# Two encoder layers on one core: statistics on TensorE, weight splits, and group D's row permutation by SBUF transfers

## The reference

```
for each of 2 layers:
  h = LN0(alpha*h + 0.5*SwiGLU_0(h))                    # D_MODEL 1024, D_FF 2816
  h = LN1(alpha*h + W_o [A(h) | B(h) | C(h) | D(h)])    # four groups of four heads
  h = LN2(alpha*h + 0.5*SwiGLU_1(h))
layer_norm: (x - mean) * rsqrt(var + eps) * g + b
group D:    cq -> rms_norm -> @ w_uq -> per head 64 plain + 32 rotated dimensions (rope)
            ckv -> rms_norm -> @ w_ukv -> keys and values; softmax over visible chunks
rope:       [x1*cos - x2*sin, x2*cos + x1*sin]          # x1, x2: the two halves of a head
```

## Time and profile before

| | |
|---|---|
| median of 3 runs | 1152.07 us (1151.99 to 1152.39) |
| the profiled execution | 1151.99 us, its span 1150.2 us |
| busy, share of the span | PE 1132.4 us, 98%; PEld 96%; DVE 60%; ACT 47%; POOL 8% |
| chain that ended last | PE 88%, DVE 7%, ACT 3%, issue 2% |
| granted TensorE clock | 9 tenths or more in all 40 slices |

### The profile page before, as it was taken

The page is one execution under the profiler, slowest core; times in us unless marked ns, Lnnn a source line. Parts: engine busy times, 40 slices in busy tenths (PEclk is TensorE's granted clock), DMA queues, the critical chain, the costliest instruction groups (busy, mean ns, idle before and its releaser), DMA issues.

```text
span 1150.2 us, 20743 instructions
## 1 busy us (share of the span) xinstructions
PE 1132.4 (98%) x8616; PEld 1099.7 (96%) x8616; DVE 684.9 (60%) x929; ACT 541.5 (47%) x770; POOL 86.4 (8%) x84
## 2 busy tenths in 40 slices
PE   9999999999999999999999999999999999999998
PEld 8999999978899999999999999999788989999997
DVE  6545445778659754545585544467777596454443
ACT  6343443464755634344373434345547565344332
POOL 1000000100161000000100000010003310000001
PEclk9999999999999999999999999999999999999999
DMA  9554444432433545444445544443433425444431
GB/s 346 184 178 151 173 146 159 165 128 91 152 114 117 211 149 182 148 163 165 148 149 189 175 157 162 165 151 117 166 109 132 150 79 216 158 171 154 159 126 42
DMA packets 28788, 178.20 MB, mean 155 GB/s; under 512 B 3568, under 2 KB 3632, under 8 KB 11056
## 3 DMA queue, kind: packets, MB, share of 16 engines
q1 hardware_dynamic: 26976, 171.36, 43.6%
q0 software_dynamic: 1744, 5.88, 1.5%
HBM read 171.79 MB, written 4.25 MB: 153 GB/s over the span
## 4 chain that ended last, share of the span: by engine, by line
PE 88%; DVE 7%; ACT 3%; issue 2%; DMA 0%; SPq 0%; ACTq 0%; DVEq 0%
PE ps L505 26%; PE ps L507 26%; PE ps L506 26%; ACT w_high L1136 2%; DVE z L1626 1%; DVE w_low L1465 1%; DVE w_low L1478 1%; PE ps L795 1%; PE ps L952 1%; PE ps L953 1%; PE ps L954 1%; DVE z L1616 1%; DVE zx_low L1606 1%; DVE x_low L1641 1%; PE ps L910 1%
## 5 line engine op out<-in xcount | busy, mean ns | idle before, releaser
L505 PE MATMUL ps<-x_high,w_high 128*128 128x288 f32 x1536 | 455.5, 297 | 3.9 <-DVE w_low L1465 3.1
L507 PE MATMUL ps<-x_high,w_low 128*128 128x288 f32 x1536 | 453.1, 295 | 0.0
L506 PE MATMUL ps<-x_low,w_high 128*128 128x288 f32 x1536 | 453.1, 295 | 0.0
L1465 DVE TENSOR_TENSOR w_low<-raw,w_high 128x2048 fp32r<-128x2048 f32 (+3 forms) x150 | 326.6, 2180 | 208.8 <-ACT w_high L1136 208.5
L1136 ACT ACTIVATE w_high<-raw 128x2048 fp32r<-128x2048 f32 (+2 forms) x166 | 302.6, 1827 | 113.8 <-PE ps L507 107.7
L505 PEld LDWEIGHTS ps<-x_high,w_high 128*128 128x128 f32 x1536 | 288.4, 188 | 8.3 <-issue 3.9
L507 PEld LDWEIGHTS ps<-x_high,w_low 128*128 128x128 f32 x1536 | 288.5, 188 | 0.0
L506 PEld LDWEIGHTS ps<-x_low,w_high 128*128 128x128 f32 x1536 | 288.3, 188 | 0.1
L505 PE MATMUL ps<-hid_high,w_high 128*128 128x288 f32 x704 | 208.4, 296 | 0.0
L506 PE MATMUL ps<-hid_low,w_high 128*128 128x288 f32 x704 | 208.0, 295 | 0.0
L507 PE MATMUL ps<-hid_high,w_low 128*128 128x288 f32 x704 | 207.9, 295 | 0.0
(11 more groups left out here) (318 smaller groups left out, 1143.2 us busy)
## 6 DMA issues: line engine op xcount, KB each, us to landing
raw<-weights SPq DMA_DIRECT2D x138, 1024.0 KB, 4.9
raw<-weights SPq DMA_DIRECT2D x16, 768.0 KB, 4.3
raw<-weights SPq DMA_DIRECT2D x4, 968.0 KB, 4.7
raw<-weights SPq DMA_DIRECT2D x6, 512.0 KB, 4.1
raw<-weights SPq DMA_DIRECT2D x8, 256.0 KB, 6.2
out_k<-kT POOLq DMA_DIRECT2D x2, 864.0 KB, 4.5
raw<-weights SPq DMA_DIRECT2D x2, 640.0 KB, 5.5
hT<-x_in SPq DMA_DIRECT2D x4, 288.0 KB, 5.5
```

The costliest lines, as they stand in the source:

```text
L505: pe.matmul(out, wh, xh, start=first, stop=False, skip_group_check=True)
L506: pe.matmul(out, wh, xl, start=False, stop=False, skip_group_check=True)
L507: return pe.matmul(out, wl, xh, start=False, stop=last, skip_group_check=True)
L1465: dve.tensor_tensor(wl, r, wh.bitcast(F32), ALU.subtract).then_inc(low_ready, 1)
```

## The change

It has four parts.

1. In norms 0, 2 and 3 VectorE adds tile 7 to both sums (two more adds, a new semaphore `all_squares_ready`), and TensorE's statistics are two matmuls in place of four. Ahead of an FFN and of the mixer a second early tile stands in front of the statistics (`EARLY_FFN` 2; for norms 1 and 4 it was 2 already). In norms 0 and 3 the first value chunk is split in two halves, one ahead of `scale(0)` and one behind tile 3, and `token_major` waits for them apart.
2. In the mixer the sum of ckv's squares is done behind tile 13 in place of 14, and ScalarE's `latent_rstd(1)` stands ahead of two copies.
3. Group D's rows are exchanged by eight SBUF-to-SBUF transfers of 16 rows, issued by SyncE. They write into `cq_x`, whose own contents are done with by then. TensorE's permutation matmul goes, and rope_b reads SBUF in place of PSUM.
4. In norms 1, 2 and 4 ScalarE makes the w_high of the next FFN's fourth chunk ahead of the last x_high, and VectorE its w_low ahead of the three reads of `early_gate`. The gate and up products of an FFN's tile 3 go to PSUM banks 2 and 3, and two waits of TensorE ahead of them go.

```diff
-EARLY_FFN, EARLY_MIX = 1, 2
+EARLY_FFN, EARLY_MIX = 2, 2
...
-BY_PE = 3
-D_SWAP = 1
+BY_PE = 2
...
         def gate_bank(t):
-            return (0, 6, 4)[t % 3]
+            return 2 if t == 3 else (0, 6, 4)[t % 3]
...
+        def sums_whole(n):
+            return n in EARLY and n % 3 != 1
...
+            def turn_rows_d(l):
+                sp.wait_ge(d_copied, 4 * l + 2)
+                sp.wait_ge(latent_low_ready, 2 * l + 1)
+                for b in range(8):
+                    other = b + 1 - 2 * (b % 2)
+                    sp.dma_start(cq_x[16 * b:16 * b + 16, 0, :], rope_x[16 * other:16 * other + 16, 0, 0, :])\
+                        .then_inc(d_turned, 16)
...
                         if local == WO_AT + 3:
                             turn_rows(l, 3)
+                            turn_rows_d(l)
                         load(l, local, 0)
...
-                    pe.wait_ge(gated_ready, 1)
...
-                    pe.wait_ge(early_read, early_before(event - 1) + 1)
...
                 pe.wait_ge(zsum_ready, n + 1)
+                if sums_whole(n):
+                    pe.matmul(mean, ones, zsum[:, 0, :], start=True, stop=True).then_inc(mean_ready, 1)
+                    pe.wait_ge(all_squares_ready, whole_before(n) + 1)
+                    pe.matmul(square, ones, zsqsum[:, 0, :], start=True, stop=True).then_inc(stat_ready, 1)
+                    for k in range(first, KD):
+                        early_tile(n, k)
+                    return
...
-                    if k % 4 == 0:
+                    if k == 0:
+                        pe.wait_ge(half_low_ready, early_before(event - 1) + 1)
+                    if k in (2, 4):
                         pe.wait_ge(low_ready, l * LAYER_CHUNKS + TM_AT + k // 4 + 1)
...
-                    if t == 14:
+                    if t == 13:
                         pe.wait_ge(o_low_ready, 4 * l + 1)
                         pe.wait_ge(latent_squared, 2 * (l + 1))
                         pe.matmul(ps[:, 1, 0:TOK], ones, ckv_sq, start=True, stop=True).then_inc(latent_summed, 1)
...
-                pe.wait_ge(d_copied, 4 * l + 2)
-                pe.matmul(ps[:, D_SWAP, 0:TOK], swap_r, rope_x[:, 0, 0, :], start=True, stop=True).then_inc(swapped, 1)
...
-                        if which == 0 and j == 3:
+                        if j == (3 if which == 0 else 6):
                             high_until(next_chunks(n) + NSPLIT + 1)
...
                 softmax(l, 0, 0.125)
+                latent_rstd(1)
                 to_rope(3, 0)
                 to_rope(3, 1)
-                latent_rstd(1)
...
                     n = 3 * l + 2 * i - 1
+                    low_until(base + 1 + NSPLIT)
                     dve.wait_ge(chunk_used, base + 1)
...
                     dve.wait_ge(early_read, early_before(n) + 1)
-                    low_until(base + 1 + NSPLIT)
...
+                    if at_ == 7 and sums_whole(n):
+                        dve.wait_ge(z_ready, 5 * (n + 1))
+                        dve.tensor_tensor(zsum[:, 0, :], zsum[:, 0, :], z[:, 7, :], ALU.add).then_inc(zsum_ready, 1)
+                        dve.wait_ge(zsqsum_ready, n + 1)
+                        dve.wait_ge(zsq_ready, 5 * (n + 1))
+                        dve.tensor_tensor(zsqsum[:, 0, :], zsqsum[:, 0, :], zsq[:, 1, :], ALU.add)\
+                            .then_inc(all_squares_ready, 1)
...
-                if n in EARLY and which == 0:
-                    low_until(next_chunks(n) + NSPLIT)
-                if n in EARLY and which > 0:
+                if n in EARLY:
                     low_half(next_chunks(n) + 2, 0, half_low_ready)
...
-                    if n in EARLY and which > 0 and j == 4:
+                    if n in EARLY and j == (3 if which == 0 else 4):
                         low_half(next_chunks(n) + 2, 1)
...
-                dve.wait_ge(swapped, BY_PE * (l + 1))
-                link(dve.tensor_tensor(rope_b[:, 0, :], ps[:, D_SWAP, 0:TOK], tab[:, 1, 0, :], ALU.mult))
+                dve.wait_ge(d_turned, 8 * 16 * (l + 1))
+                link(dve.tensor_tensor(rope_b[:, 0, :], cq_x[:, 0, :], tab[:, 1, 0, :], ALU.mult))
```

More of the change, by code:

```diff
@@ L253, in encoder_program @@
         zsum_ready, zsqsum_ready = sem("zsum_ready"), sem("zsqsum_ready")
+        all_squares_ready = sem("all_squares_ready")
         mean_ready, stat_ready = sem("mean_ready"), sem("stat_ready")
@@ L267, in encoder_program @@
         swapped, rows_turned = sem("swapped"), sem("rows_turned")
+        d_turned = sem("d_turned")
         roped = sem("roped")
@@ L323, in last_bank, with whole_before @@
             return (0, 1, 6, 7, 4)[j - BY_DVE]
-        def ffn_before(n):
-            return sum(m % 3 > 0 for m in EARLY if m < n)
+        def sums_whole(n):
+            return n in EARLY and n % 3 != 1
+        def whole_before(n):
+            return sum(sums_whole(m) for m in range(n))
         def squares_added(n, q):
@@ L538, in first_two @@
                         if t == 2 and k == 0:
-                            pe.wait_ge(half_low_ready, ffn_before(event - 1) + 1)
+                            pe.wait_ge(half_low_ready, early_before(event - 1) + 1)
                         if k == (0, 4)[t - 1]:
@@ L1568, in residual @@
                         dve.wait_ge(z_ready, 5 * n + 4)
-                        dve.tensor_tensor(zsum[:, 0, :], zsum[:, 0, :], z[:, 6, :], ALU.add).then_inc(zsum_ready, 1)
+                        ins = dve.tensor_tensor(zsum[:, 0, :], zsum[:, 0, :], z[:, 6, :], ALU.add)
+                        if sums_whole(n):
+                            link(ins)
+                        else:
+                            ins.then_inc(zsum_ready, 1)
+                    if at_ == 7 and sums_whole(n):
[5 more added lines that the diff above has]
+                            .then_inc(all_squares_ready, 1)
                 zq = z[:, 2 * q:2 * q + 2, :]
```

## The result

The changed kernel takes 1162.68 us (median of 4 executions, 1162.53 to 1163.45), the kernel before on the same chip 1152.03 (1151.98 to 1152.39): ratio 1.0093, 95% interval 1.0080 to 1.0105. It is slower by 10.65 us; forecast were +4.3 and at most +7.3. The profiled execution took 1162.81, its span is 1160.9, 10.7 longer than before.

A forecast was written before the change was run, and what follows sets the result against it. TensorE, busy 98% of the span at full clock, was taken as the bound, so only its work or 18 us not busy could change. Terms -1.7 + 5.0 + 0.6 + 0.4 = +4.3 on 1151.99 gave 1156.3 us, range 1152.6 to 1159.3.

The forecast's parts named there:

- Part 1: Norms 0 and 3: fewer statistics matmuls and a half split bring the first normalised tile sooner, -0.85 us a norm, -1.7 in all.
- Part 2: Mixer's latent sum: 1.1 us sooner, nearly all waited out at group A's value product; 0.2 left, worth nothing after group D.
- Part 3: Group D: eight issues at 0.6 us, then rope_b and qd_rot held by GpSimd; TensorE +2.5 a layer, +5.0 in all.
- goes on: Group D, behind the qd_rot wait: TensorE goes on at 317.65 in place of 315.13, +2.5 us a layer.
- Layer 1 repeats it: Whole kernel: the same TensorE waits come in both layers, so everything was told of layer 0 alone.
- Part 4: Split behind norms 1, 4 and 2: the late silu chain costs +0.3 us each for 1 and 4, +0.4 for norm 2.

The follow-up runs named there:

- pool_late: The changed kernel, with GpSimd starting its splits only when qd_rot is done: 1153.87 us.
- parts_1_2: As no_d, and the split behind norms 1, 2 and 4 put back where it was before: 1152.99 us, ratio 1.0016.
- no_d: The changed kernel without group D's transfers; TensorE turns the rows again and rope_b reads PSUM: 1152.37 us, ratio 1.0011.
- two_queues: The changed kernel, with four of group D's eight transfers issued by ScalarE in place of SyncE: 1153.87 us.
- after_shift: The changed kernel, with six matmuls of 16 columns added in layer 0 in front of the wait for qd_rot: 1161.97 us.
- d_alone: The kernel before, with group D's transfers alone added: 1163.62 us.
- part_1: The kernel before with only the statistics and half split; equally parts_1_2 with the latent's sum at tile 14, its rstd behind the copies: 1151.17 us, ratio 0.9993.
- parts_1_2_store_late: As parts_1_2, with GpSimd's store of the keys issued behind its first split chunk in place of ahead of it: 1161.33 us, ratio 1.0081.

## Why the prediction was wrong

- **Part 1, right.** TensorE is 0.89 ahead behind norm 0, 0.1 of it from before the norm; norm 3 won 0.80. Forecast were 0.85 each.
- **Part 2, right on TensorE's path** (of 1.07 won, 0.24 were left at line 1070; forecast 0.2), but its side effect was not seen: with VectorE's kT sooner, GpSimd's store came up close behind the fourth row transfer and VectorE came sooner to what waits for it, and a delay of those transfers now counts.
- **Part 3, the wait right, the price of it wrong.** The eight issues took 5.01 us, 0.63 each, the last landed at 313.90, rope_b and qd_rot took 1.20 and 1.40, and TensorE lost 2.65 where 2.5 was forecast. That the landing fits to 0.1 us is in part luck: an issue took a little more than the 0.6 that was taken, and the last transfer landed 1.86 after its issue, not 2.1. The step that failed is that TensorE "goes on" behind the wait as before: it goes on at half clock, and 2.7 us more are lost in layer 0. The prediction named the granted clock once, as full, and never asked what a wait of 3 us would do to it, though the longest wait of TensorE in the kernel before was 1.2. Of the two things that it said could move the time, TensorE's work and its idle time, neither is this one: the same work took longer. At 2.7 in each layer this term would have made +5.0 into +10.4.
- **"Layer 1 repeats it" failed.** There the fetch delayed other transfers, TensorE lost 5.6 us at line 1070 in place of 0.4, and 1.3 from there to the masks, at half clock. Layer 1 lost 1.2 us more in group D than layer 0.
- **Part 4, right.** Norms 1 and 4 lost 0.28 each (forecast 0.3), norm 2 0.34 (forecast 0.4). One reading was wrong without harm: TensorE's wait behind norm 1 in the kernel before is 0.61, and shrinks to 0.06; the 0.9 of the earlier trace rows stands in the mixer.

The terms as measured: -0.85, -0.24, +2.65 and +2.70 for layer 0's norm, latent, wait and clock; +0.28 and +0.34 for norms 1 and 2; -0.80 for norm 3; +6.36 from there to layer 1's masks; +0.28 for norm 4. Sum 10.7, the span's difference (the first of them holds the 0.1 from before norm 0).

## What to carry to other kernels

A wait of TensorE has two prices: its own length, and the work behind it at half clock if the clock falls in it or just behind it; in layer 0 here 2.65 and 2.70 us. The second price is not fixed: behind waits of 3.1 us for qd_rot it was 1.5 in one run and 3.0 in another. Ask of every new wait whether it is longer than any that the trace shows TensorE to survive at full clock. Where a step waits for transfers, count the issues in a row on one queue (eight at 0.63) before their size, and leave a margin between such transfers and both a large store and whoever waits for them: with the store's issue 0.2 us (layer 0) and 0.5 us (layer 1) behind the last of them the executions spread over 8 to 9 us where the profile shows a fetch on them and over 1.5 to 1.8 where it shows none; with 0.7 and 1.1 they spread over 2.

## What the runs showed of the hardware that was not expected

- Waits for qd_rot of 3.1 and 4.3 us brought TensorE's clock to half for 6.8 and 10.2 us in layer 0, and waits of 1.39 (pool_late), 1.68 (parts_1_2) and 1.77 (no_d) left it full. Two layers with waits of some 2 us (pool_late and two_queues, layer 1) show 3.4 us at half. The length of the wait alone does not tell the rest: 3.1 us were followed by 6.8 us at half in after_shift's layer 1 and by 3.4 in d_alone's, and in both the clock fell only when TensorE had been at work again for 0.6 and 1.4 us.
- A 16 KB instruction fetch lengthened the second of four issues from 0.59 to 1.3 to 1.6 us in all six profiled kernels in which it began within 0.15 us of that issue, and six matmuls more in the layer before moved it away. In part_1 it began 0.4 us behind the fourth issue, and that transfer landed 3.16 us after its issue in place of 2.1. What the fetch shares with SyncE's issue the traces do not show.
- In parts_1_2_store_late a VectorE instruction on 128x4 elements took 5.27 us in either layer and ended with the last of four GpSimd pieces in a row; no other in these runs took over 1.35 us more than the shortest of its kind, which is about one piece. It began 0.3 us ahead of the first piece, when GpSimd had just issued its store, whose packets came 5.0 us after the issue in place of some 1.4. Whether the pieces or the store held it is open.
